# Reordering the recurrence's key factors, norms and head sums, and turning latent keys and queries between query projections and the memory's heads

## What is computed

```python
# first layer of the second block
p_tm = p_tm + (token_shift(p_tm) - p_tm) * a_shift_mu[i]
r, k, v, d_lo, a_lo, g_lo = jnp.split(p_tm, RWKV_SPLITS, axis=-1)
lr = jax.nn.sigmoid(a_aaa_bias[i] + a_lo @ a_aaa_up[i])
gate = jax.nn.sigmoid(g_lo) @ a_gate_up[i]
kk = l2_normalize(heads(k * a_k_k[i], RWKV_HEADS))      # inverse norms, 12 heads
k = k * (1.0 + (lr - 1.0) * a_k_a[i])                   # the key factor
y = rwkv7_scan(rh, heads(decay, RWKV_HEADS), kh, vh, -kk, kk * lrh)
y = head_group_norm(y, a_lnx_g[i], a_lnx_b[i])
y = y + jnp.sum(rh * kh * a_r_k[i], axis=-1, keepdims=True) * vh   # the head sums
m = memory_attention(heads(q_mem, MEM_HEADS), mem_n, a_mem_kv[i])  # attention "m0"
# second layer
kv = (c_kv @ kv_w_up).reshape(bsz, s_len, 12, 64 + 64)  # 12 latent heads
q = (c_q @ b_q_up[j]).reshape(bsz, s_len, 12, 64 + 32)  # jobs bq0, bq1, bq2
q_rope = rope(q[..., 64:], cos[:, :, None, :], sin[:, :, None, :])
o = causal_mla_attention(q_nope, q_rope, k_nope, k_rope, v_mla)    # attention "l"
m = memory_attention(heads(q_mem, MEM_HEADS), mem_n, b_mem_kv[j])  # attention "m1"
```

## Time and profile before

| what | us |
|---|---|
| median of three runs | 1232.4 |
| the profiled execution, its own time | 1233.31 |
| its span, first to last instruction | 1232.0 |
| PE busy | 1175.4 |
| DVE busy | 756.6 |
| ACT busy | 576.2 |

### The profile page before, as it was taken

The page is one execution under the profiler, slowest core; times in us unless marked ns, Lnnn a source line. Parts: engine busy times, 40 slices in busy tenths (PEclk is TensorE's granted clock), DMA queues, the critical chain, the costliest instruction groups (busy, mean ns, idle before and its releaser), DMA issues.

```text
span 1232.0 us, 21998 instructions
## 1 busy us (share of the span) xinstructions
PE 1175.4 (95%) x9617; PEld 1094.4 (89%) x9617; DVE 756.6 (61%) x962; ACT 576.2 (47%) x770; POOL 63.1 (5%) x135
## 2 busy tenths in 40 slices
PE   7998999999999999898789999999999899999998
PEld 6777778779999999887688999999987779999998
DVE  4555866556565556756786676555575666555553
ACT  5444665346444344555352545344365464544343
POOL 2310020000000000200000000000010000000000
PEclk9998999999999999998899999999999899999999
DMA  6941344423555545522100355555544105555541
GB/s 258 338 152 69 137 171 154 154 103 138 178 199 174 198 176 185 184 103 103 35 3 3 101 187 173 194 181 182 195 171 171 69 1 173 192 183 181 196 173 68
DMA packets 30235, 185.00 MB, mean 150 GB/s; under 512 B 3579, under 2 KB 6848, under 8 KB 9148
## 3 DMA queue, kind: packets, MB, share of 16 engines
q1 hardware_dynamic: 24464, 174.07, 39.5%
q0 software_dynamic: 2464, 7.11, 1.9%
q10 hardware_dynamic: 3212, 2.42, 0.6%
HBM read 180.18 MB, written 3.41 MB: 149 GB/s over the span
## 4 chain that ended last, share of the span: by engine, by line
PE 78%; DVE 9%; ACT 7%; issue 3%; DMA 2%; POOL 0%; ACTq 0%; SPq 0%; DVEq 0%
PE bank L625 75%; ACT w_hi L2115 3%; DVE w_lo L1369 2%; DMA w_raw<-in_weights 2%; PE bank L799 1%; ACT exps L2205 1%; DVE stats L1549 1%; PE bank L772 1%; ACT x_channels_hi L2166 1%; DVE inverse_rms_rows L1484 1%; DVE logits L1541 1%; PE bank L639 1%; DVE inverse L2006 0%; ACT mem_squares L2121 0%; DVE inverse_t L2030 0%
## 5 line engine op out<-in xcount | busy, mean ns | idle before, releaser
L1369 DVE TENSOR_TENSOR w_lo<-w_raw,w_hi 128x2048 fp32r<-128x2048 f32 x160 | 364.7, 2291 | 225.2 <-ACT w_hi L2115 225.0
L2115 ACT ACTIVATE w_hi<-w_raw 128x2048 fp32r<-128x2048 f32 x164 | 311.7, 1913 | 109.8 <-DMA w_raw<-in_weights 104.5
L625 PE MATMUL bank<-x_channels_hi,w_hi 128*128 128x256 f32 x1232 | 200.7, 286 | 3.2 <-DVE memory_queries L1859 2.0
L625 PE MATMUL bank<-x_channels_lo,w_hi 128*128 128x256 f32 x1232 | 198.5, 284 | 0.0
L625 PE MATMUL bank<-x_channels_hi,w_lo 128*128 128x256 f32 x1232 | 192.6, 279 | 0.0
L625 PEld LDWEIGHTS bank<-x_channels_hi,w_hi 128*128 128x128 f32 x1232 | 170.5, 192 | 6.7 <-issue 3.1
L625 PEld LDWEIGHTS bank<-x_channels_lo,w_hi 128*128 128x128 f32 x1232 | 168.7, 191 | 0.1
L625 PEld LDWEIGHTS bank<-x_channels_hi,w_lo 128*128 128x128 f32 x1232 | 166.7, 190 | 0.0
L625 PE MATMUL bank<-hidden_hi,w_lo 128*128 128x256 f32 x528 | 103.4, 284 | 0.0
L625 PE MATMUL bank<-hidden_hi,w_hi 128*128 128x256 f32 x528 | 102.1, 281 | 0.4 <-ACT hidden_hi L2353 0.4
L625 PE MATMUL bank<-hidden_lo,w_hi 128*128 128x256 f32 x528 | 101.8, 280 | 0.0
(11 more groups left out here) (421 smaller groups left out, 1657.2 us busy)
## 6 DMA issues: line engine op xcount, KB each, us to landing
w_raw<-in_weights SPq DMA_DIRECT2D x164, 1024.0 KB, 4.8
bias_rows<-bias_lines POOLq DMA_DIRECT2D x3, 768.0 KB, 4.4
mem_rows<-in_mem POOLq DMA_DIRECT2D x2, 1024.0 KB, 6.0
bias<-bias_rows ACTq DMA_DIRECT2D x1, 1536.0 KB, 13.5
xn<-in_x SPq DMA_DIRECT2D x1, 1024.0 KB, 5.1
out<-xn SPq DMA_DIRECT2D x4, 256.0 KB, 2.2
wide_masks<-in_triangle_masks POOLq DMA_DIRECT2D x1, 832.0 KB, 6.6
bias<-bias_rows ACTq DMA_DIRECT2D x1, 768.0 KB, 4.9
```

Source lines behind the costliest of these rows:

```text
L625: return nc.tensor.matmul(out, lhs, rhs, start=start, stop=stop)
L1369: V.tensor_tensor(k.w_lo[:, s, :], k.w_raw[:, s, :], k.w_hi[:, s, :].bitcast(F32), ALU.subtract).then_inc(k.lo_done, 1)
L2115: A.activation(k.w_hi[:, s, :], k.w_raw[:, s, :], ACT.Copy).then_inc(k.hi_done, 1)
```

## The change

1. **Ahead of the recurrence, ACT.** The six `key_factor` activations move up, from behind the two decay exponentials to behind the squares. The square root moves ahead of the three gate copies. Both decay exponentials move ahead of the `keep_pair`s of `ain3` and `ain4`.
2. **The same, DVE and PE.** The reciprocal moves ahead of the second `raw_pair(3)`. `raw_pair(4, 0)` and `shift_pair(4, 0)` move behind the `removal_key` products. PE makes the `norms` between the two blocks of `projection(4, 0)`.
3. **Recurrence.** The head sums (`rk`) are made after six heads of chunk products and not after four. `shift_pair(5, 0)` moves behind the second inverse. The `rows` pieces move from levels 1 and 2 to levels 2 and 3.
4. **Latent heads.** The gathering of keys, the rotation of queries (now in three parts: heads 0 to 4, 5 to 9, 10 and 11) and the twelve turns and copies move into `m1`'s turns. The 24 `warm` transposes there are gone. The split of the unit that follows (`product("bq2", 0)` on ACT and DVE) moves from `m1`'s fourth turn to behind `m1`. All values of `m1` go to PSUM bank 3.

```diff
+LATENT_TURNS = [("k", 0, 2), ("k", 1, 2), ("k", 2, 2), ("k", 3, 4), ("k", 4, 2), ("k", 5, 5), ("q", 0, 4), ("q", 1, 2), ("q", 2, 5),
+                ("q", 3, 4), ("q", 4, 6), ("q", 5, 7)]
+QUERY_PARTS = [(0, 5), (5, 10), (10, 12)]
...
     def values_bank(self, tag, j):
-        return 3 if tag == "m0" else 2 + j % 2
+        return 3 if tag in ("m0", "m1") else 2 + j % 2
...
     for level in range(1, LEVELS + 1):
         order += [("first", 0, level), ("first", 1, level)]
-        order += [("rows", 2 * level - 2, 0)] if level < 3 else []
+        order += [("rows", 2 * level - 4, 0)] if 2 <= level < 4 else []
...
         order += [("second", 0, level), ("second", 1, level)]
-        order += [("rows", 2 * level - 1, 0)] if level < 3 else []
+        order += [("rows", 2 * level - 3, 0)] if 2 <= level < 4 else []
...
@@ PE, beside m1 @@
     def beside_m1(i):
+        if i == 3:
+            turn_heads(1, k.ht_v.at("l", 0))
         if 1 <= i + 1 < len(ups):
             kept(ups[i])
             product(ups[i + 1], 0, L if ups[i + 1][0] == "k" else Q, "lat" if ups[i + 1][0] == "k" else "qlat")
...
+        if i == 2:
+            turn_heads(0, k.act_once.all("kcat"), k.pool_once.all("k_rot"))
+        if i == 3:
+            turn_heads(2, k.ht_a.at("l", 0))
+        if i == 4:
+            turn_heads(3, k.exped.at("m1", 2))
+            turn_heads(4, k.ht_v.at("l", 1))
+            turn_heads(5, k.exped.at("m1", 3))
+            turn_heads(6, k.dve_once.at("q_turned", 1), k.ht_a.at("l", 1))
+            turn_heads(7, k.ht_v.at("l", 2))
+        if i == 5:
+            turn_heads(8, k.dve_once.at("q_turned", 3), k.ht_a.at("l", 2))
...
+            turn_heads(11, k.dve_once.at("q_turned", 5), k.pt.at("m1", 3))
     attention("m1", beside_m1)
-    PE.wait_ge(*k.exped.all("m1"))
-    PE.wait_ge(*k.pt.all("m1"))
-    warm(8, 6)
...
     PE.wait_ge(*k.o.all("m1"))
-    warm(10, 2)
...
-    warm(6, 2)
     PE.wait_ge(*k.ht_v.all("l"))
     PE.wait_ge(*k.ht_a.all("l"))
     attention("l", lambda i: warm(8, 0) if i == 0 else None)
...
@@ PE, recurrence @@
-    projection(4, 0)
-    PE.wait_ge(*k.dve_once.at("nrm", 1))
+    def norms(m_):
+        if m_:
+            return
+        PE.wait_ge(*k.dve_once.at("nrm", 1))
...
+    projection(4, 0, norms)
...
-        if h == 4:
+        if h == 6:
             PE.wait_ge(*k.dve_once.at("rk", 0))
...
@@ DVE, beside m1 @@
     def beside_m1(i):
-        if i < len(last):
-            rows_of(last[i])
+        if i >= len(last):
+            for n in ((4, 6), (8, 10))[i - len(last)]:
+                heads_copied("l", n, k.latent_heads(n), QK)
+            return
+        rows_of(last[i])
+        if i >= 2:
+            heads_copied("l", 2 * (i - 2), k.latent_heads(2 * (i - 2)), QK)
+        if i:
+            h0, h1 = QUERY_PARTS[i - 1]
+            V.wait_ge(*k.rows_a.all(last[i]))
+            V.wait_ge(*k.rows_v.all(last[i]))
+            rotate(queries[:, :, h0:h1, 64:96], h1 - h0, "q_turned", i - 1)
+        if i < 3:
             product(last[i], 0)
     attention("m1", beside_m1)
...
+    product("bq2", 0)
     attention("l")
...
@@ DVE, recurrence @@
     raw_pair(3, 0)
-    raw_pair(3, 1)
     V.wait_ge(*k.act_once.at("sqrt", 0))
     V.reciprocal(k.nrm[:, :], k.nrm[:, :]).then_inc(k.dve_once.sem, 1)
+    raw_pair(3, 1)
     shift_pair(3, 0)
     shift_pair(3, 1)
     product("ain4", 0)
-    raw_pair(4, 0)
-    shift_pair(4, 0)
...
     V.tensor_tensor(kB, kB, k.fac[:, :, :], ALU.mult).then_inc(k.dve_once.sem, 1)
+    raw_pair(4, 0)
     V.tensor_tensor(lr[:, :, :], kk[:, :, :], lr[:, :, :], ALU.mult).then_inc(k.dve_once.sem, 1)
+    shift_pair(4, 0)
...
         turn(half)
-        shift_pair(5, half)
+    shift_pair(5, 0)
+    shift_pair(5, 1)
...
@@ ACT, beside m1 @@
+        if i >= len(last):
+            for n in ((3, 5, 7), (9, 11))[i - len(last)]:
+                heads_copied("l", n, k.latent_heads(n), QK)
+            return
+        if i == 3:
+            heads_copied("l", 1, k.latent_heads(1), QK)
+        rows_of(last[i])
+        if i < 3:
             product(last[i], 0)
...
     attention("m1", beside_m1)
...
+    product("bq2", 0)
     attention("l")
```

More of the change, by code:

```diff
@@ L291, in rw_signals @@
         self.pool_once = Signal(nc, "pool_made", ident=1, half=1, ones=2, blocks=1, less=2, sig0=1, reset=1, causal=1, k_rot=2)
-        self.act_once = Signal(nc, "act_made", table=2, lam=1, tanh=2, sig=6, lr=6, squares=1, gate=3, sqrt=1, e1=1, e2=1, factor=1, rk=3,
+        self.act_once = Signal(nc, "act_made", table=2, lam=1, tanh=2, sig=6, lr=6, squares=1, factor=1, sqrt=1, gate=3, e1=1, e2=1, rk=3,
                                gated=1, v=8, sin=1, abs=1, cos=1, kcat=2)
@@ L561, in heads_bank, with latent_heads @@
             return 4 + n % 2
-        return {"mk0": 4, "mk1": 5, "m1": 6}.get(stage, 4 + n % 6 % 4)
+        if stage == "l":
+            return LATENT_TURNS[n][2]
+        return {"mk0": 4, "mk1": 5, "m1": 6}.get(stage, 4 + n % 4)
+    def latent_heads(self, n):
+        which, pair, _ = LATENT_TURNS[n]
+        return (self.k96 if which == "k" else self.q96)[:, 2 * pair:2 * pair + 2, :]
     def scale_of(self, tag):
@@ L1065, in tensor_program, with turn_heads @@
     ups = ["kvu0", "kvu1", "bq0", "bq1", "bq2"]
+    def turn_heads(n, *freed):
+        which, pair, b = LATENT_TURNS[n]
+        for sem, value in freed:
+            PE.wait_ge(sem, value)
+        rows = k.kcat if which == "k" else k.qr
+        for j, (h, tok) in enumerate((h, tok) for h in (2 * pair, 2 * pair + 1) for tok in range(NT)):
+            m = nc.tensor.transpose(bank[b][0:QK, j * P:(j + 1) * P], rows[:, tok, QK * h:QK * (h + 1)], ident)
+        m.then_inc(k.ht_turned.sem, 1)
     def beside_m1(i):
+        if i == 3:
+            turn_heads(1, k.ht_v.at("l", 0))
         if 1 <= i + 1 < len(ups):
@@ L1787, in vector_program, with rotate @@
     channels_lo("qlat", (0, 1))
-    def rotate(src, heads, stage):
+    def rotate(src, heads, stage, part=0):
         for tok in range(NT):
-            if tok:
+            if tok or part:
                 V.wait_ge(*k.dve.so_far())
-                V.wait_ge(*k.dve_once.at(stage, 0))
+                V.wait_ge(*k.dve_once.at(stage, 2 * part + tok - 1))
             cb, sb_ = (x[:, tok, :].unsqueeze(1).to_broadcast((P, heads, 16)) for x in (k.cosr, k.sinr))
@@ L2469, in recurrence_scalar @@
     a.then_inc(k.act_once.sem, 1)
-    product("ain3", 1)
-    for n in range(3):
-        A.wait_ge(*k.pe_once.at("gate", n))
-        A.activation(k.gate[:, n, :, :], bank[4 + n][:, :].rearrange("p (k t) -> p k t", k=2), ACT.Copy).then_inc(k.act_once.sem, 1)
-    A.wait_ge(*k.dve_once.at("nrm", 0))
-    A.activation(k.nrm[:, :], k.nrm[:, :], ACT.Sqrt).then_inc(k.act_once.sem, 1)
-    keep_pair(3, 0)
-    keep_pair(3, 1)
-    product("ain4", 0)
-    keep_pair(4, 0)
-    A.wait_ge(*k.dve_once.all("scans"))
-    A.activation(k.down[:, :, :, :], k.cs[:, :, :, :], ACT.Exp, scale=-KAPPA, bias=k.middle[:, 0:1]).then_inc(k.act_once.sem, 1)
-    A.wait_ge(*k.act_once.at("e1", 0))
-    A.activation(k.up[:, :, :, :], k.cs[:, :, :, :], ACT.Exp, scale=KAPPA, bias=k.middle[:, 1:2]).then_inc(k.act_once.sem, 1)
+    A.wait_ge(*k.act_once.all("lr"))
     for b in range(RWB):
@@ L2488, in recurrence_scalar @@
     a.then_inc(k.act_once.sem, 1)
+    product("ain3", 1)
+    A.wait_ge(*k.dve_once.at("nrm", 0))
+    A.activation(k.nrm[:, :], k.nrm[:, :], ACT.Sqrt).then_inc(k.act_once.sem, 1)
+    for n in range(3):
+        A.wait_ge(*k.pe_once.at("gate", n))
+        A.activation(k.gate[:, n, :, :], bank[4 + n][:, :].rearrange("p (k t) -> p k t", k=2), ACT.Copy).then_inc(k.act_once.sem, 1)
+    A.wait_ge(*k.dve_once.all("scans"))
+    A.activation(k.down[:, :, :, :], k.cs[:, :, :, :], ACT.Exp, scale=-KAPPA, bias=k.middle[:, 0:1]).then_inc(k.act_once.sem, 1)
+    A.wait_ge(*k.act_once.at("e1", 0))
+    A.activation(k.up[:, :, :, :], k.cs[:, :, :, :], ACT.Exp, scale=KAPPA, bias=k.middle[:, 1:2]).then_inc(k.act_once.sem, 1)
+    keep_pair(3, 0)
+    keep_pair(3, 1)
+    product("ain4", 0)
+    keep_pair(4, 0)
     product("ain5", 0)
```

65 lines of the change are left out of this document (22 added, 43 removed).

## The result

The changed kernel takes 1244.39 us, median of 20 executions (1233.76 to 1247.27). The kernel before, run beside it, takes 1235.8 us, median of 20 (1232.29 to 1239.78). The ratio is 1.0042, interval [1.0024, 1.006]. It is smaller than the quotient of the medians (1.0070), because the times of the changed kernel fall into two groups and the median lies in the larger one; the means, 1241.16 and 1235.56, give 1.0045. The forecast was 1232.5 with a range to 1237.5, so it was wrong, and on the wrong side.

What follows compares the result with a forecast made beforehand. PE, busy 1175.4 of 1232.0 us, was taken as the bound, so the change acts only where PE waits or runs at low clock. +0.65 − 0.9 + 0.4 = +0.15 on 1232.4 gave 1232.5 us, range 1227 to 1237.5.

Steps and rivals of the forecast that it cites:

- The base: Time of the kernel before from which the forecast was counted: 1232.4 us, the median of the runs shown.
- Part 1, ahead of m0: Items 1 and 2: removal keys end later behind load, exponentials, kept shares and a w_lo; m0 starts 0.65 us later.
- first rival: Ahead of m0: removal keys come first, PE's 4.14 idle and the low clock behind it go; 1226.8 us, chance 0.08.
- Part 1 by the Trainium skill: Ahead of m0: a drain of about 1.38 us besides the table load would make part 1 +2.0; not used.
- Part 2: Item 3, recurrence: later head sums and shifts, rows products moved to better-covered levels; 0.9 us faster, bounds -1.8 and 0.5.
- What was to show it: Sign for item 3 in the recurrence: sixth pair of head products about 1.5 us earlier, counted from m0's start.
- Part 3, up to the first masked logits: Item 4, m1 to attention l: turns end earlier but w_hi and w_lo follow the last copies; l starts 0.5 us sooner.
- Part 3, behind the gap: In attention l: low clock after PE idles about 4 us; 0.9 us slower, bounded by 0 and 3.
- The slower one: Rival, last latent copy to first masked logits: late w_hi and w_lo, l's first heads at low clock; 1235.65 us, chance 0.17.
- what the prediction calls slower: Whole kernel: a measured time above 1238.6 us, beyond the 0.5% a measurement can tell; chance 0.05.

Runs made afterwards that it cites:

- part 1 alone: Kernel before with only the recurrence's key factor, norms and exponentials in the new order (items 1 and 2); 1237.18 us, ratio 1.0024.
- part 2 alone: Kernel before with only the head sums, shifts and rows moved (item 3); 1233.19 us, ratio 0.9985.
- split early: Changed kernel with the w_hi and w_lo of product("bq2", 0) put back beside m1's heads; 1231.36 us, ratio 0.9971.
- the late split: Kernel before with only the bq2 split moved behind the latent copies, the 24 unread transposes kept; 1247.97 us, ratio 1.0089.
- second run of the changed kernel: Changed kernel measured again without any edit; 1245.18 us, ratio 1.0063 against the kernel before.
- part 3 alone: Changed kernel with items 1 to 3 taken back, only the latent heads (item 4) changed; 1244.58 us, ratio 1.006 against the kernel before.

## Why the prediction was wrong

- *The base.* The forecast was counted from 1232.4, the median of three executions; twenty beside the changed kernel gave 1235.8. Of the 11.9 us between 1232.5 and 1244.39, 3.4 are this base. The change itself moved the median by 8.6, where 0.15 was forecast.
- *Part 1, ahead of m0 (+0.65).* Right for the start of m0: +0.67 in part 1 alone, by the chain that the prediction named, the w_lo "only because of its place" included. (The rows as written there end at 569.1, 0.7 and not 0.65 behind 568.38.) The kernel's time moved more, 1.4 to 4.4 us by the ratio. The sum had no term for the low clock behind the wait, which I had weighed as a gain in the first rival (5.1 for wait and clock together) and not as a cost when the wait grew. From m0's first to its second logits it is about 0.5 on average; where the rest comes from stays open. That rival's condition was never met by the change, but its price was about right: with w_lo and shares moved, part 1 is worth 0.33%, some 4 us.
- *Part 1 by the Trainium skill.* ScalarE: Activation LUTs, "What ACT_TABLE_LOAD costs", would have put a drain of about 1.38 us beside the load. The trace doesn't agree: in the changed kernel too the load of 1.28 starts at 555.80, right behind a copy that ends at 555.79, and the exponential starts at 557.10.
- *Part 2 (-0.9).* Right in sign and place, somewhat small: -1.65 in the profile, 0.9985 in the ratio (-3.6 to 0 us). What was to show it was too large: counted from m0's start, the sixth pair came 0.88 sooner in part 2 alone, and in the changed kernel 0.2 sooner (lower group) and 0.3 later (upper group), and not 1.5 sooner.
- *Part 3, up to the first masked logits (-0.5).* Right in mechanism. The late wait of 2.58 ahead of m1's last transposes, the w_lo right before the masked logits and the 3.74 of idle were forecast within 0.3 us. The gain wasn't there: counted from m1's first logits, the masked logits come 0.2 later in the lower group's profile and 0.2 sooner in the upper one's.
- *Part 3, behind the gap (+0.9): the step that failed.* "I charge 0.9 for that in attention l, bounded by 0 and 3." From the first masked logits to the turn of l's output it is 27.83 before, 28.78 in the lower group (+0.95) and 39.50 in the upper one (+11.7), and 11 of 20 executions belong to the upper group. The bound was read from m0, where the clock came back within 8 us behind a wait of this kind, in before and in part 1 alone. I carried it over to a stretch of 36 us of attention, and in the upper group it didn't come back there. Three facts show that the gap is the cause: taking it away (split early) and filling it (36 transposes, all work as late as before) both remove the upper group, and making it alone in the kernel before brings the group in.
- *The rivals.* The slower one had the right place and mechanism, "take over attention l", and the same bound of 3 for the clock: it ended at 1235.65. With the stretch's whole length at the low clock, 12 heads by 1.06 more (3.20 less 2.14), its price would have been 12.7 and not 3. The 3.20 was not known then, but before's own rows gave an estimate: PE is busy for 21.20 of the 24 us between 984 and 1008, and four logits at the low clock took 2.07 and not 1.13. So these 24 us would become about 39.
- *The chances.* By the median the result is what the prediction calls slower (above 1238.6), and I gave 0.05 to that; by the ratio it is 0.42%, under its 0.5%. The range held only the lower group. That this group, at a median of 1234.74, lies so near the kernel before is in part luck: part 1 cost more and part 2 brought more than forecast.

What stays open is what decides between the groups in one execution. In the profiles of the lower and the upper group both have the same instructions, the same 3.74 us gap and a low clock ahead of it (0.65 and 0.57 from 964 to 972), and the clock is at 1.00 when the gap begins. The four profiles that were read differ in when the clock falls. In both of the lower group it holds until the gap ends (at 983.52 in the changed kernel, 983.67 in the late split); in both of the upper group it is already at 0.50 within the gap (which ends at 982.35 in the second run of the changed kernel, 983.49 in part 3 alone). Windows in this order:
```profile
983.20:983.50 0.30, 0.00 (x0) 0.00 (x0) 0.30 (x2) 0.27 (x2) 0.00 (x0) 0.98 0.00 0
```
```profile
983.35:983.65 0.30, 0.00 (x0) 0.00 (x0) 0.30 (x3) 0.26 (x2) 0.00 (x0) 1.00 0.00 0
```
```profile
982.05:982.35 0.30, 0.00 (x1) 0.01 (x1) 0.30 (x3) 0.24 (x2) 0.00 (x0) 0.50 0.00 0
```
```profile
982.25:983.15 0.90, 0.00 (x0) 0.00 (x0) 0.87 (x4) 0.70 (x3) 0.00 (x0) 0.50 0.00 0
```
Two profiles of each group are too few to call this the cause. No run has a gap of another length, so how short it must be to be harmless isn't known either.

Over the four runs with the late split and an unfilled gap, 18 executions were in the lower group and 32 in the upper (20, 12, 12 and 6 executions). Over the nine other changed kernels, in 91 executions, none was above 1240.1. Of the 50, four profiles were read (two of each group); for the other executions the group is told by time and mean clock alone.

## What to carry to other kernels

When a wait on PE grows or appears, price what follows it as well as the wait: take the whole stretch that follows and what it would take with PE at the low clock. That is the upper bound, and not what the clock cost at another place. A conversion that nobody needs yet doesn't belong between the last copy and the first reduction of an attention; put it beside the heads before, or behind what PE waits for. And look at single executions, not only at a median: a kernel that is sometimes 10 us slower shows it there first. The same holds for profiles: the time of a stretch with an unchanged order differed by 1.2 us between three of them, so a difference of that size in one pair shows nothing yet.
